# Where the modulation vector is computed, and in which order ScalarE empties the attention's banks, in a two-block transformer on one core

## The reference, cut to what matters

```python
def _fox_attend(q_blk, c_q, pos_q, k, v, c_k, pos_k):
    s = jnp.einsum('bhqd,bhkd->bhqk', q_blk, k).astype(jnp.float32) * (FOX_HEAD_DIM ** -0.5)
    s = s + (c_q[..., :, None] - c_k[..., None, :])
    s = jnp.where(pos_k[None, :] <= pos_q[:, None], s, -jnp.inf)
    p = jax.nn.softmax(s, axis=-1)
    return jnp.einsum('bhqk,bhkd->bhqd', p, v.astype(jnp.float32))
...
def swiglu(h, w_in, w_out):
    gate, up = jnp.split(h @ w_in, 2, axis=-1)
    return ((jax.nn.silu(gate) * up) @ w_out).astype(h.dtype)
...
        mod = jax.nn.silu(c) @ w_ada[i] + b_ada[i]
        sh1, sc1, g1, sh2, sc2, g2 = jnp.split(mod[:, None, :], 6, axis=-1)
        n1 = _rmsnorm(h, norm1_g[i]) * (1.0 + sc1) + sh1
```

## Time and profile before

| what | us |
|---|---|
| median of 3 runs | 2527.92 (2524.71 to 2528.28) |
| the profiled execution's own time | 2522.89 |
| its span | 2521.1 |
| PE busy | 2326.7 (92% of the span) |
| DVE, ACT, POOL busy | 909.0, 738.7, 770.6 |

### The profile page before, as it was taken

One profiled execution on the slowest core, in us unless ns is written; L12 is line 12 of the kernel. 1 busy time (PEld: TensorE's weight loads), 2 busy tenths in 40 slices (PEclk: granted clock), 3 DMA queues, 4 the chain that ended last, 5 costly groups with the idle time before them and its releaser, 6 DMA issues.

```text
span 2521.1 us, 26948 instructions
## 1 busy us (share of the span) xinstructions
PE 2326.7 (92%) x11046; PEld 1440.0 (57%) x11046; DVE 909.0 (36%) x1584; ACT 738.7 (29%) x1181; POOL 770.6 (31%) x488
## 2 busy tenths in 40 slices
PE   8999989999999999999999998988888889889885
PEld 5677557788887788778776884323222223223321
DVE  2634552100005699946776334211111111111113
ACT  3434562332223333348676322100000000001001
POOL 3233653454554344343333630211111010000100
PEclk9999999999999999999999998999999999999997
DMA  5344313423323433334334448999999999999996
GB/s 174 110 155 153 103 46 134 167 93 108 100 76 109 101 101 84 125 119 138 134 117 148 188 172 314 424 424 424 424 424 425 427 426 425 425 426 426 426 427 257
DMA packets 174202, 597.33 MB, mean 237 GB/s; under 512 B 17669, under 2 KB 96517, under 8 KB 148352
## 3 DMA queue, kind: packets, MB, share of 16 engines
q1 hardware_dynamic: 154992, 562.23, 57.3%
q10 hardware_dynamic: 8416, 23.92, 2.4%
q0 software_dynamic: 10672, 9.46, 1.1%
HBM read 591.02 MB, written 28.97 MB: 246 GB/s over the span
## 4 chain that ended last, share of the span: by engine, by line
PE 56%; DMA 27%; DVE 11%; ACT 4%; issue 1%; SPq 0%; POOL 0%; ACTq 0%; DVEq 0%; POOLq 0%
DMA arena<-in_w 17%; PE ps L785 11%; PE ps L787 11%; PE ps L786 11%; DMA ring<-in_w 9%; PE ps L1332 7%; DVE ps L2238 5%; PE ps L1330 3%; PE ps L1351 2%; PE ps L812 1%; PE ps L867 1%; ACT arena L1434 1%; PE ps L985 1%; PE ps L836 1%; ACT L1434 1%
## 5 line engine op out<-in xcount | busy, mean ns | idle before, releaser
L2686 POOL TENSOR_TENSOR ring_r<-ring,ring_r 128x1024 fp32r<-128x1024 f32 x220 | 515.5, 2350 | 677.5 <-ACT ring_r L1423 677.4
L785 PE MATMUL ps<-r,ring_r 128*128 128x512 f32 (+1 forms) x1536 | 610.7, 398 | 1.3 <-DVE arena L2226 1.2
L787 PE MATMUL ps<-r,ring_r 128*128 128x512 f32 (+1 forms) x1536 | 598.7, 390 | 0.0
L786 PE MATMUL ps<-r,ring_r 128*128 128x512 f32 (+1 forms) x1536 | 598.4, 390 | 0.0
L1434 ACT ACTIVATE arena<-ps 128x512 f32<-128x512 f32 (+4 forms) x274 | 183.3, 687 | 1130.7 <-PE ps L1332 855.3
L1332 PE MATMUL ps<-arena 128*64 128x512 f32 x672 | 317.5, 628 | 70.7 <-DMA arena<-in_w 70.4
L785 PEld LDWEIGHTS ps<-r,ring_r 128*128 128x128 f32 (+1 forms) x1536 | 287.0, 187 | 77.3 <-issue 13.9
L1330 PE MATMUL ps<-arena 128*64 128x512 f32 x688 | 329.8, 627 | 0.0
L786 PEld LDWEIGHTS ps<-r,ring_r 128*128 128x128 f32 (+1 forms) x1536 | 287.1, 187 | 64.1 <-issue 4.3
L787 PEld LDWEIGHTS ps<-r,ring_r 128*128 128x128 f32 (+1 forms) x1536 | 286.9, 187 | 63.0
L1423 ACT ACTIVATE ring_r<-ring 128x1024 fp32r<-128x1024 f32 x220 | 222.9, 1015 | 319.4 <-PE ps L787 214.5
(11 more groups left out here) (357 smaller groups left out, 2460.5 us busy)
## 6 DMA issues: line engine op xcount, KB each, us to landing
arena<-in_w SPq DMA_DIRECT2D x106, 2048.0 KB, 35.6
ring<-in_w SPq DMA_DIRECT2D x86, 2048.0 KB, 37.3
ring<-in_w_ada SPq DMA_DIRECT2D x12, 2048.0 KB, 8.1
ring<-in_ffn_w_in SPq DMA_DIRECT2D x22, 1024.0 KB, 7.7
ring<-in_w_in SPq DMA_DIRECT2D x40, 512.0 KB, 6.4
ring<-in_w_in SPq DMA_DIRECT2D x8, 2048.0 KB, 9.1
ring<-in_fox_w_in SPq DMA_DIRECT2D x7, 2048.0 KB, 10.0
arena<-acs_d SPq DMA_DIRECT2D x16, 512.0 KB, 3.5
```

The costliest lines, as they stand in the source:

```text
L785: e.matmul(out, wh[:, k, :], X.hi[:, k0 + k, :], start=first and k == 0, stop=False)
L786: e.matmul(out, wh[:, k, :], X.lo[:, k0 + k, :], start=False, stop=False)
L787: m = e.matmul(out, wl[:, k, :], X.hi[:, k0 + k, :], start=False, stop=last and k == nk - 1)
L2686: e.tensor_tensor(GL[t], grans[t][1], GH[t].bitcast(F32), ALU.subtract).then_inc(sem["gr_lo"], 1)
```

## The change

It does two things.

1. In the attention, ACT's program in step m has the copies of the transposes of m-2 first and the exponentials of m behind them (before, the other way round).
2. The modulation vector is taken off PE. DVE computes it, in the feed-forward part only: for block n, 8 instructions multiply the 8 slices of the block by a number per partition and add them up in two sums that take turns (`AD[0]`, `AD[1]`), and a ninth adds the two into `ADS`. The 12 products stand behind the multiplications of hidden tiles 0, 2, 4, 6, 8, 10 (blocks 0 to 5), behind output tiles 0, 2, 4, 6 of the first half (6 to 9), and behind hidden tiles 12 and 14 (10 and 11). PE's `ada_columns(n)` now sums `ADS` over the partitions with a column of ones, as many tiny matmuls as before, and stands one even tile later. All twelve are in the feed-forward part. ACT has no copy for them. In the list of loads the blocks of `w_ada` leave the attention part and alternate with the weights from the first hidden tile to tile 14, and SP swaps none. `NCK0`, a buffer in the ring, moves to the other slot.

```diff
+def ada_after(nt):
+    return (nt // 2 + 4 * (nt > 11),) if nt % 2 == 1 and 0 < nt < 16 else ()
+def ada_between(half, nt):
+    return (6 + nt // 2,) if half == 0 and nt % 2 == 1 else ()
+def ada_done(half, nt):
+    return (9,) if nt == 12 else ada_after(nt - 1)
+def ada_out(half, nt):
+    return (5,) if (half, nt) == (0, 0) else ada_between(half, nt - 1)
...
     for k0, n in HALVES:
         for nt in range(k0, k0 + n, 2):
             two(a["ffn_w_in"], 128 * nt, FH + 128 * nt)
-            if nt < 8:
-                ada(8 + nt // 2)
+            for i in ada_after(nt + 1):
+                ada(i)
...
+            for i in ada_between(k0 // 12, 2 * c + 1):
+                ada(i)
...
-            return [(ps("ada", n).full, ps("ada", n).n + 1)]
+            return [(sem["adv"], n + 1)]
...
-            def ada(n):
-                u = ps("ada", n)
-                i, aw = ada_load[n]
-                w.wait_ge(loads[i].slot, loads[i].value)
-                w.wait_ge(sem["sc"], 1)
-                w.wait_ge(u.free, u.n)
-                for k in range(8):
-                    g = k % 4
-                    m = e.matmul(u.ap[32 * g:32 * g + 32], SC[:, k:k + 1].broadcast_to([128, 32]), aw[:, k, :], start=k < 4, stop=k >= 4)
+            def ada_columns(n):
+                u = ps("adb", n)
+                w.wait_ge(sem["adv"], n + 1)
                 w.wait_ge(u.free, u.n)
+                for j in range(4):
+                    m = e.matmul(u.ap[:, j:j + 1], ADS[:, j * 128:(j + 1) * 128], ones[:, 0:1], start=True, stop=True)
                 m.then_inc(u.full, 1)
...
             for m in range(32 + 3):
-                if m < 32:
-                    ln = NM + 128 * (m % 4 + 1)
-                    for hh in range(2):
-                        pb, n = PB[m % 3][hh][:, :ln], 2 * m + hh
-                        w.wait_ge(sem["pmax"], n + 1)
-                        e.activation(pb, pb, ACT.Exp, bias=NMX[:, n:n + 1], accum_out=SUM[:, n:n + 1]).then_inc(sem["pexp"], 1)
                 if 2 <= m < 34:
                     u = ps("t", m - 2)
...
                     evict(PTM[m % 2], u, ACT.Copy, src=cols(u.ap[0:NM, 0:256], 2))
+                if m < 32:
+                    ln = NM + 128 * (m % 4 + 1)
+                    for hh in range(2):
+                        pb, n = PB[m % 3][hh][:, :ln], 2 * m + hh
+                        w.wait_ge(sem["pmax"], n + 1)
+                        e.activation(pb, pb, ACT.Exp, bias=NMX[:, n:n + 1], accum_out=SUM[:, n:n + 1]).then_inc(sem["pexp"], 1)
...
+            def ada(n):
+                i, aw = ada_load[n]
+                w.wait_ge(sem["sc"], 1)
+                w.wait_ge(loads[i].slot, loads[i].value)
+                for k in range(8):
+                    acc = AD[k % 2]
+                    if k < 2:
+                        e.tensor_scalar(acc, aw[:, k, :], SC[:, k:k + 1], None, ALU.mult).then_inc(d.next(), 1)
+                    else:
+                        two_back()
+                        e.scalar_tensor_tensor(acc, aw[:, k, :], SC[:, k:k + 1], acc, ALU.mult, ALU.add).then_inc(d.next(), 1)
+                last()
+                e.tensor_tensor(ADS, AD[0], AD[1], ALU.add).then_inc(sem["adv"], 1)
...
-            order = list(range(len(loads)))
-            for n, (i, _) in ada_load.items():
-                if n in (5, 6) or n >= 8:
-                    order[i - 1], order[i] = i, i - 1
```

113 lines of the change are left out of this document (25 added, 88 removed).

## The result

| | median of the runs, us | ratio to the kernel before, 95% interval |
|---|---|---|
| before, beside the changed kernel | 2526.53 (2524.71 to 2528.28, 4 runs) | |
| changed | 2509.11 (2508.59 to 2512.09, 4 runs) | 0.9928 [0.9916, 0.9940] |
| before, in the later batch | 2527.63 (2524.31 to 2530.28, 8 runs) | |
| changed, measured again beside it | 2507.56 (2505.20 to 2508.79, 5 runs) | 0.9920 [0.9906, 0.9934] |

A ninth run of the kernel before in the later batch fell in a slower state of the chip (3269 us at a granted clock of 0.65) and is left out. The change is worth 17 to 20 us. The forecast of 35.6 us was about twice that, and the time lies above the range's top of 2508.

What follows compares the result with a forecast made beforehand. PE, busy 92% of the span, was taken to bound the kernel up to 812 us, DMA the experts. -29.6 on PE, +5.0 feed-forward and -11 attention gave -35.6 us: 2487.3 from the profiled 2522.9, 2492 for the median; range 2485 to 2508.

Steps and rivals of the forecast that it cites:

- the products' price on PE: Ahead of the feed-forward part: blocks 0 to 3 leaving K and V save PE 14.7 us, blocks 4 to 8 14.9 us.
- The attention's mechanism and period: Attention: copies first let PE start transposes without waiting for ACT; four steps take about 12.8 us instead of 14.2.
- The single slot at hidden tile 2: Feed-forward part: the weights' one slot makes granule 4 ready at 465.6 when PE wants it at 464.1, costing 1.6 us.
- The experts' length: Experts' stretch, bound by the DMA: it moves earlier and keeps the same length.
- its own signs of being wrong: PE waits above 2 us in each output-tile block, attention starting less than 20 us earlier, or waits for POOL's scaling there.
- I charge nothing (bound: 4 us): K and V: DVE's chain of norms starts from PE's own product and moves with it, so no loss; at most 4 us.
- Attention, -11: Attention: ACT's copies first save 11 us, bounds 6 and 13.4, from eight groups of four steps.
- exponentials behind copies: Attention: exponentials stand behind up to 1.26 us of copying, 0.8 us later at steps with 272 keys; reason for 11, not 13.4.
- Spare: 0.4 us: Output tiles: POOL is done at 16.9 of 17.3 us in four blocks; 1.2 us loss taken, including the step back to hidden tiles.
- +5.0: Feed-forward part: three products leaving PE -6.2 us, nine more column groups +8.4, losses +2.8.
- the product's 5.8 us on DVE: Feed-forward part: two scalings 0.99 us, six multiply-adds 4.06, an addition 0.69 and some gap, from a second-block convolution.
- the rival at 0.06: Output tiles: POOL splits take turns with DVE's instructions, products last 6 us longer, weights issue late; +24 us, 2516; chance 0.06.

Runs made afterwards that it cites:

- its variant: The kernel before with only ACT's copies of the transposes put ahead of the exponentials in the attention; 2518.48 us (0.9964).

## Why the prediction was wrong

Three steps failed: nothing was charged in V, a product was priced at 5.8 us on DVE also beside POOL's splits, and the sum has no term for TensorE's clock. The attention was mis-sized within its bounds.

**Right.** The direction, and the products' price on PE: K, the Q and G stages and the output projection gave 25.6 us where 26.0 was charged. The attention's mechanism and period, 12.64 against "about 12.8", and no PE wait for ACT's copies. The single slot at hidden tile 2: 1.9 to 2.7 us for 1.6. The experts' length. Of its own signs of being wrong two came, both narrowly: the attention started 19.9 us earlier, not 23 to 24, and PE waited for POOL's scaling in it (1.8 us). A wait above 2 us came in one block of output tiles, not in each.

**"I charge nothing (bound: 4 us)".** The norms in V cost 3.7 us of that bound. The step said that DVE's chain moves with PE's product. It does, and so PE's wait of 1.7 us stayed. What failed is the sentence behind it, that the early loads get both slots "which takes no time away": a slot that comes free 45 us sooner puts a split where DVE is busy with two-input instructions, and that adds 2.07 us. The other 1.6 us is the clock behind the longer pause: with fillers and the same split the stage lost just that.

**Attention, -11.** Measured -8.4, within the bounds of 6 and 13.4. The reason that was given for taking 11 (exponentials behind copies) was not the one: 2.7 us go at the start, 1.2 of them to rows behind a weight block; where the other 1.5 go was not tested.

**"Spare: 0.4 us", loss 1.2.** The feed-forward part was +10.6, not +5.0. The term that failed is the product's 5.8 us on DVE. Taken from a chain that kept its 0.68 us each, it didn't hold beside a POOL batch: 10.8 us in the case shown. The same trace had six such chains, and the one 22 us ahead of the chosen one shows the other outcome:

```profile
1165.94 6.19 DVE L2199 SCALAR_TENSOR_TENSOR arena<-arena,params_sb 128x512 f32<-128x512 f32 x6
1168.22 2.70 POOL L2686 TENSOR_TENSOR ring_r<-ring,ring_r 128x1024 fp32r<-128x1024 f32 x1 [4.16 <-ACT ring_r L1423]
```

Six multiply-adds took 6.19 us there, the one behind the split 2.87 by itself; the forecast read one chain of six and set the rival at 0.06. (In the chain that it read, the split ended 2.3 us behind DVE's, not 2.4.) The rival of splits between DVE's instructions described what came, with a product of about 12 us and weights issued right behind a modulation block. But its price of 24 us was wrong too: among the output tiles it came to one PE wait, of 2.5 us. By the rule of the Trainium skill that the prediction quoted (SBUF — State Buffer, Who interferes with whom), the port goes to one instruction at a time, and the multiply-adds of 2.87, 2.89 and 1.78 us behind splits agree with that against the forecast's reading of the earlier trace rows. That reading's own chain, 0.74 us for each record while a split lasted 4.21 us, is the case in which POOL didn't come in between; which of the two happens no run here explains. The sum: columns less products +2.2, waits 4.4, and 6.8 us at 1.2 GHz for at most 3.4, together at most 10.0 of 10.6.

**No term for the clock.** The sum has nothing for time at 1.2 GHz, and gives no reason. This is the largest part: 31 us more of it in the profiled pair, up to 15 us of time, and 22 us more in the mean of three profiles each, up to 11 us, of the 15 to 18 us by which the forecast was too high. The shares named above for V and the feed-forward part are in it. The windows of before hinted at it only weakly: their 0.99 ahead of the attention comes from the first 30 us, and their 0.96 among the experts from a stretch that the DMA bounds. Some of it was the luck of the profiled execution: its own time stood 5 us under the median, and the forecast carried that difference over as if it were the same for both kernels. The V stage shows it as a cost with all else equal; for the whole kernel its size is an estimate, at most half the stretches' length.

**The range.** The first measurement is 1.1 us above its top of 2508, the second 0.4 below. It had no bound for the clock, which by the estimate above was worth up to 11 us.

## What to carry to other kernels

When work leaves the busiest engine, ask of every wait that stays on it whether the engine will now pause longer there, and add the time at the lower clock behind the pause. Fillers can hide that in the one place, if they are sized from their measured duration and done before the wait is over. When a buffer comes free sooner, follow its transfer to the next engine that touches it: an earlier start can be an earlier collision, and holding that work back costs nothing if it isn't due. A duration measured in a quiet place is the lower bound in a busy one: take the price of a DVE chain from beside POOL's batches if it will run there, and read every instance of it in the trace, not one. One profile of a kernel isn't its clock: take two or three before a difference in stretches at 1.2 GHz is put down to a change.

## What the runs showed of the hardware

A pause of TensorE of 1.9 us was followed by 3.4 us at the 1.2 GHz level in one execution of a kernel, and pauses of 1.8 us in the same execution by none; among executions of the same program the places differed. The longest pause of the first block, 3.8 us in V, was followed by such a stretch in all ten profiles that had it without fillers in its place, and in neither of the two with them; the wait of 1.7 us there in the kernel before and its variant was followed by none in four. DVE's two-input instructions on 16 partitions are held up by a split on POOL as those on 128 are: seven went from 5.08 to 7.15 us, and the split among them took 2.74 us in place of 2.40. An add's record of 128x512 lasted 744 ns in an undisturbed chain, and 996 or 1196 in the mean of 72, by how much of POOL's work fell beside it; the longest took 2.9 us.
